# The filter network beside the second feed-forward block's down product, odd taps first, and the residual norm between the transform blocks

## The reference, cut to what matters

```python
h = h + 0.5 * rmsnorm(swiglu(rmsnorm(h, ffn2_pre_w), ffn2_w_gu, ffn2_w_down), ffn2_post_w)
...
k_ctx, v_ctx = context_kv(modulate(ctx, norm1_g, ch1, cs1), p)   # 256 tokens
...
h = sin(freq * (feats @ f1 + b1)); h = sin(freq * (h @ f2 + b2)); h = sin(freq * (h @ f3 + b3))
h = (h @ f4).reshape(L, 2, 2, 512) * decay         # 2 filters (orders), forward and backward taps
h = h / sum(abs(h), axis=(0, 2))                   # one factor per order and channel
kf = rfft(concat(forward, 0, reversed backward))   # 2 spectra
...
z = modulate(x, norm1_g, sh1, sc1) @ w_in + b_in
```

## Time and profile before

| | before |
|---|---|
| median of 3 runs | 3729.67 us (3727.66 to 3734.19) |
| the profiled execution | 3727.16 us, its span 3725.3 us |
| PE busy | 3532.4 us (95%) |
| PEld busy | 2996.4 us (80%) |
| DVE / ACT / POOL busy | 56% / 37% / 49% |
| from the first context matmul to the second in-projection block | 1653.5 to 1834.6 us |

### The profile page before, as it was taken

The page is one execution under the profiler, slowest core; times in us unless marked ns, Lnnn a source line. Parts: engine busy times, 40 slices in busy tenths (PEclk is TensorE's granted clock), DMA queues, the critical chain, the costliest instruction groups (busy, mean ns, idle before and its releaser), DMA issues. The chain is left out here.

```text
span 3725.3 us, 49795 instructions
## 1 busy us (share of the span) xinstructions
PE 3532.4 (95%) x17547; PEld 2996.4 (80%) x17547; DVE 2092.5 (56%) x4197; ACT 1386.8 (37%) x1941; POOL 1838.5 (49%) x909
## 2 busy tenths in 40 slices
PE   8999997999999999997988999989999999999999
PEld 5777766777787688773676766779999999999999
DVE  4653055222234344125666255459999997677776
ACT  4333234233244322222323345323345454444443
POOL 5676433233243344341333301435566676788886
PEclk9999998999999999997999999999999999999999
DMA  6997544444567299331424312685559999899996
GB/s 241 386 381 247 159 150 140 127 149 149 158 206 246 72 297 290 113 100 42 137 80 134 101 54 71 220 325 176 164 164 317 344 352 342 325 388 391 383 383 234
DMA packets 458130, 813.81 MB, mean 218 GB/s; under 512 B 31544, under 2 KB 308984, under 8 KB 455322
## 3 DMA queue, kind: packets, MB, share of 16 engines
q1 hardware_dynamic: 278416, 436.07, 35.5%
q10 hardware_dynamic: 142666, 241.11, 18.3%
q0 software_dynamic: 36864, 134.23, 9.5%
HBM read 682.84 MB, written 195.56 MB: 236 GB/s over the span
## 5 line engine op out<-in xcount | busy, mean ns | idle before, releaser
L539 POOL TENSOR_TENSOR weights_lo<-weights_raw,weights_hi 128x1024 fp32r<-128x1024 f32 x649 | 1592.7, 2459 | 1816.1 <-ACT weights_hi L1214 1692.7
L615 PE MATMUL bank<-operand_hi,weights_hi 128*128 128x512 f32 (+1 forms) x2856 | 1093.4, 383 | 54.3 <-DVE operand_lo L1916 18.7
L617 PE MATMUL bank<-operand_hi,weights_lo 128*128 128x512 f32 (+1 forms) x2856 | 1064.5, 373 | 0.0
L616 PE MATMUL bank<-operand_lo,weights_hi 128*128 128x512 f32 (+1 forms) x2856 | 1063.4, 372 | 0.0
L1214 ACT ACTIVATE weights_hi<-weights_raw 128x1024 fp32r<-128x1024 f32 x649 | 683.3, 1056 | 858.6 <-PE bank L617 559.4
L615 PEld LDWEIGHTS bank<-operand_hi,weights_hi 128*128 128x128 f32 x2856 | 541.3, 190 | 145.9 <-DVE operand_lo L1916 25.1
L616 PEld LDWEIGHTS bank<-operand_lo,weights_hi 128*128 128x128 f32 x2856 | 542.1, 190 | 74.4 <-issue 5.5
L617 PEld LDWEIGHTS bank<-operand_hi,weights_lo 128*128 128x128 f32 x2856 | 540.2, 189 | 74.7
L615 PE MATMUL bank<-expert_hi,weights_hi 128*128 128x384 f32 x1024 | 345.1, 337 | 0.0
L617 PE MATMUL bank<-expert_hi,weights_lo 128*128 128x384 f32 x1024 | 345.0, 337 | 0.0
L616 PE MATMUL bank<-expert_lo,weights_hi 128*128 128x384 f32 x1024 | 345.0, 337 | 0.0
(11 more groups left out here) (397 smaller groups left out, 4899.5 us busy)
## 6 DMA issues: line engine op xcount, KB each, us to landing
weights_raw<-in_w_ffn_gu SPq DMA_DIRECT2D x132, 512.0 KB
expert_table_v<-in_w_peer_out SPq DMA_DIRECT2D x120, 512.0 KB, 5.5
weights_raw<-in_w_peer_ahead SPq DMA_DIRECT2D x120, 512.0 KB
weights_raw<-in_w_peer_out SPq DMA_DIRECT2D x120, 512.0 KB
expert_table_u<-expert_turned ACTq DMA_DIRECT2D x360, 128.0 KB, 4.7
expert_rows<-in_w_peer_ahead ACTq DMA_DIRECT2D x82, 512.0 KB, 6.7
peer_gates<-gate_stage SPq DMA_DIRECT2D x24, 1024.0 KB
expert_gates<-peer_gates ACTq DMA_DIRECT2D x16, 1536.0 KB
```

The lines of the kernel that those rows point to most:

```text
L539: pool.tensor_tensor(LO[:, slot, :], RAW[:, slot, :], HI[:, slot, :].bitcast(F32), ALU.subtract).then_inc(sem("lo_ready"), 1)
L615: pe.matmul(out, wh, hi(k), start=(k == 0), stop=False)
L616: pe.matmul(out, wh, lo(k), start=False, stop=False)
L617: ins = pe.matmul(out, wl, hi(k), start=False, stop=(k == kc - 1))
```

## The change

- The three layers of the filter network move into the down product, after its blocks 2, 3 and 4 (`LAYER_AFTER`). Their four small weights are loaded at its start. `f4` now loads behind the decay, when the product has ended.
- Every context block is followed by a filter tile of order 0 (and from block 2 on by a norm matmul); DVE's chunk of `post` gets the tile's taps behind it. PE and DVE wait for the decay and `f4` behind context block 0.
- The transforms begin with blocks 5 to 8, from the odd taps, which need neither the reciprocal nor the skip gain; then 0 to 4. SP loads their units in that order (`DFT_UNITS`). Even taps are taken in the order 1, 2, 3, 0 and added in place.
- Order 1 has its own taps (`filter_forward1`, `filter_backward1`), and its sum a bank of its own, so its odd and even taps are made while order 0 is still transformed.
- The keys' norm, the values' turn, and the residual's squares and sums stand between transform blocks. The first four chunks of the normed operand are made before the last transforms; the last four wait for their end, since they lie where the even taps' high and low parts lay.

```diff
+LAYER_AFTER = [2, 3, 4]
+DFT_ORDER = [5, 6, 7, 8, 0, 1, 2, 3, 4]
+DFT_UNITS = [7, 8, 0, 1, 2, 3, 4, 5, 6]
+EVEN_ORDER = [1, 2, 3, 0]
 BIG = 3.0e38
...
+        FW = place("f23", [64, 2, 64], F32, F0 + 6400)
...
-        FVEC = place("f_vectors", [64, 8], F32, W1 + 10240)
-        FFW = place("filter_forward", [P, TT, TOK], F32, W1 + 10304)
-        FBW = place("filter_backward", [P, TT, TOK], F32, W1 + 18496)
-        FE = place("filter_even", [P, TT, TOK], F32, W1 + 26688)
+        FFW = [place(f"filter_forward{o}", [P, TT, TOK], F32, at) for o, at in enumerate((W1 + 10304, A0 + KB * 2048))]
+        FBW = [place(f"filter_backward{o}", [P, TT, TOK], F32, at)
+               for o, at in enumerate((W1 + 18496, A0 + KB * 2048 + 8192))]
+        FO = place("filter_odd", [P, TT, TOK], F32, W1 + 26688)
...
                         sums(DC, ONES, NMEM, bank=5)
+                    if name == "ffn2" and m in LAYER_AFTER:
+                        filter_layer(LAYER_AFTER.index(m))
...
+            pe.wait_ge(sem("sin_ready"), 3)
+            for m in range(8):
+                block_(DC, lambda k: CXH[:, k, :], lambda k: CXL[:, k, :], width=NMEM)
+                if m == 0:
+                    pe.wait_ge(sem("decay_loaded"), 48)
+                filter_tile(0, m)
+                if m >= 2:
+                    filter_norm(0, m - 2)
+            freed_context = n["freed"]
+            filter_norm(0, 6)
+            filter_norm(0, 7)
+            filter_tile(1, 0)
+            filter_tile(1, 1)
+            after = {(0, 5): [("tile", 2), ("tile", 3)], (0, 6): [("norm", 0), ("norm", 1)],
+                     (0, 7): [("tile", 4), ("tile", 5)], (0, 8): [("norm", 2), ("norm", 3)],
+                     (0, 0): [("tile", 6), ("tile", 7)], (0, 1): [("norm", 4), ("norm", 5)],
+                     (0, 2): [("norm", 6), ("norm", 7)], (0, 3): [("pair", 0)], (0, 4): [("pair", 1)],
+                     (1, 5): [("residual", 0)], (1, 6): [("residual", 2)],
+                     (1, 7): [("turn", 0), ("turn", 1), ("residual", 4)], (1, 8): [("residual", 6)]}
             for o in range(2):
                 ready = pieces_of(2 * TT)
-                for m in range(KB):
-                    e0 = 0 if m < 5 else 4
-                    block_(TT, lambda k: EOH[:, e0 + k, :], lambda k: EOL[:, e0 + k, :],
-                           ready=(lambda k: ready(e0 + k)) if m in (0, 5) else None)
-
-                    if o == 0 and m < TT:
-                        filter_tile(1, 2 * m)
-                        filter_tile(1, 2 * m + 1)
-                    if o == 0 and 1 <= m <= TT:
-                        filter_norm(1, 2 * m - 2)
-                        filter_norm(1, 2 * m - 1)
-
-
-            sums(DC, ONES, TOK)
+                for m in DFT_ORDER:
+                    e0 = 4 if m < 5 else 0
+                    block_(TT, lambda k: EOH[:, e0 + (EVEN_ORDER[k] if e0 else k), :],
+                           lambda k: EOL[:, e0 + (EVEN_ORDER[k] if e0 else k), :],
+                           ready=(lambda k: ready(e0 + k)) if m in (0, 5) else None,
+                           order=EVEN_ORDER if e0 else None)
+                    for what, i in after.get((o, m), ()):
+                        if what == "tile":
+                            filter_tile(1, i)
+                        elif what == "norm":
+                            filter_norm(1, i)
+                        elif what == "pair":
+                            sum_pair(PAIR, 6)
+                        elif what == "turn":
+                            if i == 0:
+                                pe.wait_ge(sem("block_free"), freed_context)
+                            turn([CVF[:, c, i * P:(i + 1) * P] for c in range(4)])
+                        else:
+                            sum_piece(i, bank=5)
+                            sum_piece(i + 1, bank=5)
+
...
+                    for i in range(len(UT)):
+                        act.wait_ge(sem(f"table_stored_f2{i}"), 64 * len(TABLE["f2"]) // len(UT))
+                    act.wait_ge(sem("hidden_ready"), 2 * FC)
+                    for dst, name_ in ((FTS, "feats"), (FW1, "f1"), (FW, "f23"), (FVEC, "fvec")):
+                        act.dma_start(dst[:], a[name_]).then_inc(sem("filter_weights_loaded"), 16)
...
+                    if name == "ffn2" and m in LAYER_AFTER:
+                        act.wait_ge(sem("angle_ready"), LAYER_AFTER.index(m) + 1)
+                        act.activation(FX[:], FA[:, 0, :], ACT.Sin).then_inc(sem("sin_ready"), 1)
...
-            for dst, name in ((FTS, "feats"), (FW1, "f1"), (FW, "f23"), (FW4, "f4"), (FVEC, "fvec")):
-                act.dma_start(dst[:], a[name]).then_inc(sem("filter_weights_loaded"), 16)
             act.dma_start(DCY[:], a["decay"]).then_inc(sem("decay_loaded"), 16)
+            act.dma_start(FW4[:], a["f4"]).then_inc(sem("decay_loaded"), 16)
             act.dma_start(SKIP[:], a["skip"]).then_inc(sem("decay_loaded"), 16)
             root(TOK)
...
+            for m in range(8):
+                blocks(1)
+                filter_abs(0, m)
...
+            highs(EOH[:, 0:4, :], FO, 4)
+            transforms(1)
+            filter_abs(1, 0)
+            filter_abs(1, 1)
+            even_highs(0)
+            filter_abs(1, 2)
+            filter_abs(1, 3)
+            transforms(1)
+            filter_abs(1, 4)
+            filter_abs(1, 5)
...
+            for c in range(2):
+                square(CK[:, c, :], NMEM, "block_free", kept + c + 1)
...
+            highs(EOH[:, 0:4, :], FO, 4)
+            transforms(1)
+            root(TOK, 64, 6, CKR[:, 0, :])
...
+            act.wait_ge(sem("pe_steps"), UNIT * START["hyk"] + TT * KB)
+            even_highs(1)
+            root(TOK, 64, 6, FAB[:, 0, :], table=False)
...
+            root(TOK, bank=5)
+            transforms(1)
+            highs(XH, XF2, 4, lambda c: MOD[:, c, 0:1])
+            transforms(1)
...
+            act.wait_ge(sem("pe_steps"), UNIT * n["unit"])
+            highs(XH, XF2, 4, lambda c: MOD[:, c, 0:1], 4)
...
+                        copy_blocks(YT, 1, FC, first=m, scaled=True)
+                        if m in LAYER_AFTER:
+                            layer_angle(LAYER_AFTER.index(m))
                     rstd()
...
+                if c == 0:
+                    dve.wait_ge(sem("decay_loaded"), 48)
+                filter_taps(0, c)
...
+            def odd_taps(o):
+
+                dve.wait_ge(sem("abs_ready"), 8 * (o + 1))
+                link(dve.memset(FBW[o][0:1, 0, :], 0.0))
+                for t in range(TT):
+                    made(dve.tensor_tensor(FO[:, t, :], FFW[o][:, t, :], FBW[o][:, t, :], ALU.subtract))
+                dve.wait_ge(sem("piece_made"), n["made"])
+
+            def even_taps(o, norm):
+
+                for t in EVEN_ORDER:
+                    ins = dve.tensor_tensor(FFW[o][:, t, :], FFW[o][:, t, :], FBW[o][:, t, :], ALU.add)
+                    if t:
+                        made(ins)
+                    else:
+                        link(ins)
+                sums = BANK[4 if o else 7]
                 dve.wait_ge(sem("abs_used"), 8 * (o + 1))
-
-                link(dve.tensor_tensor(SKIP[0:1, o, :], SKIP[0:1, o, :], BANK[7][0:1, :], ALU.mult))
-                dve.reciprocal(norm[:], BANK[7][:]).then_inc(sem("norm_read"), 1)
+                link(dve.tensor_tensor(SKIP[0:1, o, :], SKIP[0:1, o, :], sums[0:1, :], ALU.mult))
+                made(dve.tensor_tensor(FFW[o][0:1, 0, :], FFW[o][0:1, 0, :], SKIP[0:1, o, :], ALU.add))
+                dve.reciprocal(norm[:], sums[:]).then_inc(sem("norm_read"), 1)
                 dve.wait_ge(sem("norm_read"), o + 1)
...
+            odd_taps(0)
+            filter_taps(1, 0)
+            filter_taps(1, 1)
+            lows(EOL[:, 0:4, :], FO, EOH[:, 0:4, :], 4)
+            even_taps(0, RSTD)
+            filter_taps(1, 2)
+            filter_taps(1, 3)
+            even_lows(0)
+            transformed(0, 5)
+            filter_taps(1, 4)
...
+            odd_taps(1)
+            transformed(0, 1)
+            lows(EOL[:, 0:4, :], FO, EOH[:, 0:4, :], 4)
+            transformed(0, 2)
+            even_taps(1, MS)
+            transformed(0, 3)
+            transformed(0, 4)
+            evacuated()
+            even_lows(1)
+            context_normed(0)
+            context_normed(1)
+            for m in range(5, KB):
+                transformed(1, m)
+            evacuated()
...
+            for c in range(4):
+                made(dve.scalar_tensor_tensor(XF2[:, c, :], HT[:, c, :], COEF[:, 0, c:c + 1], RSTD[:],
+                                              ALU.mult, ALU.mult))
+            lows(XL, XF2, XH, 4, lambda c: MOD[:, c, 0:1])
+            transformed(1, 0)
```

237 lines of the change are left out of this document (104 added, 133 removed).

## The result

The changed kernel took 3689.7 us in the median (3686.0 to 3695.9 in 4 runs), the kernel before 3728.7 (3726.4 to 3734.2 in 4 runs) beside it: a ratio of 0.9896 with a 95% interval of 0.988 to 0.9911. The forecast was 3680 in a range of 3669 to 3700: the side was right, and of the 48 us foreseen 39 came.

What follows compares the result with a forecast made beforehand. A 181.1 us chain of small DVE, ACT and PE steps, PE idle or at half clock in its first half, was the bound. 53.2 saved - 2.1 (POOL) - 3.4 (clock) = 47.7, from 3727.2 to 3679.5, said as 3680; range 3669 to 3700.

Steps and rivals of the forecast that it cites:

- Layers: Down product: three small filter-layer matmuls move in where PE has no idle; +3.2 us, nothing for DVE and ACT.
- The new wait: PE's first filter tile, behind context block 0, waits for decay and `f4`; PE idles 4.0 us (sign: 3 to 6).
- Clock behind it: Context stretch, around the 4.0 us gap: 6.9 us at half clock, costing 3.4 us.
- Rival 2: From the decay gap on, the clock stays at half for 37.5 us, 18.7 lost instead of 3.4: 3695; chance 0.10.
- Tiles beside the context and the chain: Behind the decay's arrival: tiles, blocks and norms to tile 7 take 33.8 us, then the chain to the first transform 6.4.
- The 2.1 for POOL: Before the first transform: one POOL split falls where DVE makes the first low parts, taking 2.1 us off the saving.
- Transforms: First transform to in-projection: PE sets the pace with 72.1 us of work; DVE's tight places cost nothing.
- The gap before the first transform: PE's gap of 1.7 to 3.8 us there may cost as much clock as the decay gap, or nothing; counted as nothing.
- In-projection block: First in-projection block finds four operand pieces made, the fifth comes 1.5 us after the last transform; takes 5.4 us.
- rival 1: DVE bounds the transforms at 80 us, short waits may bring half clock: 4 to 10 us, 3690 to 3698; chance 0.17.
- strict reading of the port rule: Transforms: two-SBUF-input DVE operations and GpSimd ones exclude each other, adding 20 us to DVE's 60: 8 more than PE's 72.
- Rival 3: Decay lands earlier, no clock is lost, POOL misses the low parts: 53 to 57 us gained, 3671 to 3674; chance 0.07.

Runs made afterwards that it cites:

- f4 first: Changed kernel, but ACT loads `f4` ahead of the decay and PE waits for `f4` alone, only DVE's taps for the decay; 3686.8 us.
- all four: Changed kernel with `f4` loaded first, residual squares earlier, three order-1 scalings before the last operand pieces, and ACT's split behind the even high parts; 3675.1 us.
- residual norm behind: Changed kernel, but the residual's squares, sums and whole normed operand stand behind the last transform, as before the change; 3698.9 us.
- layers alone: Kernel before, with only the filter layers moved into the down product, decay issued ahead of `f4`, keys' norm waiting for all context copies; 3718.7 us.

## Why the prediction was right in its side and long by a fifth

Step by step, and where the 8.6 us between 269.6 (317.3 - 47.7) and 278.2 are:

- **Layers**, +3.2: measured +3.6, with no wait of PE. "Cost nothing" for DVE and ACT beside a down block holds. +0.4.
- **The new wait**, 4.0 us: measured 2.74, released by the last of the three loads. The mechanism is right, the size 1.3 too long; the 3 to 6 us named as a sign were missed. Context to tile 0 was 6.2 instead of 7.0: -0.8.
- **Clock behind it**, -3.4: 6.8 us at half, as after the second layer before. "f4 first" took the wait and the clock away together. Rival 2 didn't come: half clock was over in 6.8 us.
- **Tiles beside the context and the chain**, 40.2 plus 3.4 and 2.1: 45.7 predicted, 44.0 measured, -1.7. The 2.1 for POOL is the term that was off here. The split did fall on the low parts, but it held up the second and not the first, for which this segment waits: it cost nothing here, and its price appeared as the 1.13 us wait inside the first transform. Without it the steps give 43.6, 0.4 short. The rest of the step is right, for a reason that I saw only in part: the round of 5.0 us keeps POOL away from DVE.
- **Transforms**, 72.1 up to the in-projection: measured 80.9, +8.8. This is the step that failed: "they hold on paper, so I cost them at nothing, and let PE set the pace". The terms are the squares' wait 2.76, the scalings' wait 1.56, the second low part 1.13, and the half clock of 6.8 us: PE's busy time here is 75.6 us against 72.3 in "all four", where no half clock is left, so 3.2. They sum to 8.7. The forecast counted DVE's list against PE's and left out ACT's, where the squares were late. The 72.1 themselves were right: without these waits, in "all four", PE took 72.3.
- **The gap before the first transform**, "as much or nothing; I take nothing": it was as much.
- **In-projection block**, 5.4: measured 7.3, +1.9. The forecast priced the last four low parts without POOL; they took 4.84 us beside a split, which held up one of them, and PE waited 1.48 us for it. Even in the kernel with all four edits the block takes 7.8.

0.4 - 0.8 - 1.7 + 8.8 + 1.9 = 8.6. Beside the steps there is a slip: 3679.5 with the 2.5 us between median and profiled execution is 3682, not 3680.

On the rivals: rival 1, DVE as the bound at 3690 to 3698, comes near in time, but its mechanism is only latent. In the changed kernel PE waited for DVE's scalings once, for 1.56 us; "residual norm behind" shows it at 4.8 us. The forecast's strict reading of the port rule had DVE busy for 80 us and 8 us slower than PE; it was busy 61.1 of 81.0 us, POOL's share in it included. Rival 3 asked for an early decay, no half clock and no POOL beside the low parts: "all four" did all this and gained 50.2 of the 53 to 57, 51.7 without its disturbance in the down product.

What each part is worth, by undoing or doing it alone: layers at least 10.2 alone; tiles between blocks 6.7 (net of the decay's wait, which they bring), residual norm between transforms 8.7, reciprocal off the chain 9.1, each taken back from the whole. That makes 34.7 of 39.1. The parts aren't independent, so the remaining 4.4 us have no owner that a run here names. The moved wait in "layers alone" may hide some of them, and the second order's own taps weren't undone alone.

## What to carry to other kernels

When work moves off one chain, write out the list of every engine that feeds the waiting one, ACT's too, in order and with what it waits for: the missing time was in short waits of 1 to 3 us that a sum of busy times does not show. Interleave small PE work into a fast stretch if the engine that follows is slowed beside POOL: the slower pace of weight splits gave DVE's operations 0.7 us instead of 2.7. Take such waits away together: one that was left (2.13, 2.76 us) had 3.4 to 6.8 us at half clock behind it, and with one wait gone half clock could appear behind another.
